# Attention state product: one full fp32 product becomes three products of split parts

## The chip, the cores and the metric

The kernel runs on one core of a Trainium2 chip. TensorE (PE) multiplies matrices, VectorE (DVE) and ScalarE (ACT) do elementwise work, GpSimd (POOL) and SyncE (SP) issue DMAs. Each engine works through its own queue in order and waits on semaphores. The metric is the device time of one execution in microseconds (us).

## The reference, cut to what matters

One layer of a hybrid backbone: a bidirectional chunkwise mLSTM (4 heads, key width 128, value width 256) and a pooling mixer, merged by sigmoid gates, then a ConvFFN. There are 128 context rows and 1024 latent rows. The part that the change touches is the output of one mLSTM step: products inside the chunk, plus the queries against the carried state:

```python
qk = jnp.einsum('bhctk,bhcsk->bhcts', qc, kc) * wts
num = jnp.einsum('bhcts,bhcsv->bhctv', qk, vc) + sc[..., None] * jnp.einsum('bhctk,bhckv->bhctv', qc, Cs)
den = jnp.sum(qk, axis=-1) + sc * jnp.einsum('bhctk,bhck->bhct', qc, ns)
```

The kernel takes the chunk as 128 rows. For each head there are 9 steps (i = 0 to 8): step 0 is the context tile, and step i takes tile i forwards (d = 0) and tile 9 - i backwards (d = 1).

## The kernel before, in words

Nearly all products are in a three-product form: an fp32 tile is rounded to fp32r ("hi", done by ACT or DVE), the rest is subtracted out on DVE ("lo", the helper `sub_hi`, L2208), and TensorE adds hi·hi, lo·hi and hi·lo. fp32r products go through in one pass. The product of the scaled queries `qs` with the state `Cst` (L1277) is the exception: it is taken in plain fp32.

The attention stage is 36 segments, one for each step e = 9h + i of the four heads. Each of them goes with one 128-column unit of the large projection ("main", 72 products of 384 columns, or the same work in 256-column pieces for values). In a segment TensorE does the scores of step i (only for i up to 4; later steps reuse cached scores in `SC`), then the main in three blocks, then `attention_values` for d = 0 and d = 1. The products of step e begin at L1273.

DVE, in each segment: the ada products of the next unit (16 operations on 128 columns, not in every segment), the lo part of a later weight unit, `gate_arguments(e + 1)` (L2350, two operations), `attention_weights(e)` (L2367 to the last `v_lo`), then `attention_outputs(e, 0)` and `(e, 1)`, which wait for the products of step e and update the state `Cst` (L2405) or, at i = 0, write the new context state `Cctx` (L2403). The products of step e wait for `attention_weights(e)`.

ACT, in each segment: the hi part of a unit, rounding of `v_hi`, then the three blocks of the main's result out of PSUM. After the first block it calls `exps()`, which takes the exponential of the gate rows of step e + 1 (L1844) and, in the segment after a head's squares were summed, the square root for that head's norm (`hm_roots`, L1808). DVE's `head_scale` (L2467) waits for this root, and it stands between `attention_weights` and `attention_outputs` of that segment (heads' steps i = 2, three times: e = 11, 20, 29). After the blocks ACT copies the scores to `SC` (L1885), and TensorE's next scores wait for that.

POOL stores `Cctx` of each head to DRAM with four DMAs (L977, L978) after step 0; in the kernel before, only the end of the kernel and the next head's write of `Cctx` wait for these stores. SP loads the gate rows `GE` of each step into one of three slots and waits for the state update three steps back.

Of the kernel before, what the change touches and what calls it, by code (L numbers as in the profile page):

```python
# [107 lines left out]
def build(nc, x_prompt, x_sample, state_C, state_n, state_m, c, c_ctx, w_ada, b_ada, g_pre_mix, g_post_mix,  # L108
# [9 lines left out]
    LS = 5  # L118
    GSLOTS = 3
    SEEN = (NT - 1) // 2  # L120
# [51 lines left out]
    loads += [("ga", d) for d in range(KD)]  # L172
    load_of = {it: w for w, it in enumerate(loads)}

    sigmoids = [it for it in loads if it[0] != "hm"]
# [86 lines left out]
    GE = place("GE", [P, GSLOTS, 2, 2, P])  # L262
    Pt_hi = place("Pt_hi", [P, 2, P], F32R)
    v_hi = place("v_hi", [P, 2, VP], F32R, at=VT0)
    v_lo = place("v_lo", [P, 2, DV], F32R, at=VT0 + (8 * VP + 31) // 32 * 32)
    a_tok = place("a_tok", [P, NT, 2, NH])
    en_tok = place("en_tok", [P, NT, 2, NH])
    ST0 = base[0]
    Cst = place("Cst", [P, 2, VW])
    Cctx = place("Cctx", [P, 2, VW])  # L270
    AT0 = base[0]
    Pt = place("Pt", [P, 2, P])
    Pt_lo = place("Pt_lo", [P, 2, P], F32R, at=AT0)
    kw_hi = place("kw_hi", [P, 2, P], F32R)
    qs = place("qs", [P, 2, P])
    SC = place("SC", [P, SEEN, 4, P])
    ada_part = place("ada_part", [P, 2, P])
    coef_rows = place("coef_rows", [32, P], at=base[0] - 1024)
# [421 lines left out]
    with nc.Block() as block:  # L700

        @block.sync
        def _(sp):
# [46 lines left out]
            for n, it in enumerate(raw_items):  # L750
                if n == 3:
                    x_load(1)
                    x_load(2)
                    mask_load()
                if n >= RS:
                    prev = raw_items[n - RS]

                    if prev[0] == "ada":
                        sp.wait_ge(ada_summed, prev[1] - ADA0 + 1)
                    else:  # L760
                        sp.wait_ge(lo_ready, prev[1] + 1)
                if it[0] == "ada":
                    src, kt = tile_cols(w_ada[0], KD, it[1] * P), KD
                else:
                    src, kt = unit_source(it[1])
                dst = raw[:, n % RS, :] if kt is None else raw[:, n % RS, 0:kt * P].rearrange("p (k c) -> p k c", c=P)
                sp.dma_start(dst, src).then_inc(landed[n % RS], 16)
                if it[0] == "unit" and 0 <= it[1] - SEG < NT * NH:
                    gates_load(it[1] - SEG)

# [169 lines left out]
        def _(pool):  # L940
# [61 lines left out]
            for w, (what, d) in enumerate(loads):  # L1002
                if w == 0:
                    pool.wait_ge(att_state, 2 * (NT * NH - 1))
                if w == 1:

                    pool.wait_ge(att_outputs, 2 * NT * NH)
                    pool.wait_ge(att_state, 2 * NT * NH)
                    pool.wait_ge(new_state_stored, 16 * 4 * NH)

                pool.wait_ge(*store_of[(what, d)])
                if w >= LS:

# [7 lines left out]
                pool.dma_start(tiles[:, w % LS, :], Z[what][d]).then_inc(tile_in[w % LS], 16)  # L1021

# [74 lines left out]
        def _(pe):  # L1097
# [159 lines left out]
            def attention_values(h, i, d):  # L1257
# [5 lines left out]
                if i == 0 and d == 0:  # L1263

                    pe.wait_ge(evac0, values_q(h))
                if i == 1 and d == 0:
                    pe.wait_ge(state_in, 64 * (h + 1))

                if e and d == 0:
# [6 lines left out]
                if i:  # L1276
                    mm = pe.matmul(ps[:, 5 + d, 0:VW], qs[:, d, :], Cst[:, d, :], start=False, stop=True)  # L1277
                if i < NT - 1:
# [313 lines left out]
        def _(act):  # L1592
# [179 lines left out]
            def sig(what, d):  # L1772
                w = load_of[(what, d)]
                act.wait_ge(tile_in[w % LS], 16 * (w // LS + 1))
                act.activation(tiles[:, w % LS, :], tiles[:, w % LS, :], ACT.Sigmoid).then_inc(sigmoids_done, 1)

# [33 lines left out]
            for m, (kind, idx) in enumerate(mains):  # L1810
# [37 lines left out]
                if kind == "q":  # L1848
                    evac_main(act, q0, qT[idx % 2], QSCALE, exps)
                elif kind == "k":  # L1850
                    evac_main(act, q0, kT[idx % 2], 1.0, exps, NB - 1 if m == SEG - 1 else 0)
                elif kind == "u":
# [11 lines left out]
                elif kind == "v":  # L1864
                    if idx == 2:

                        act.wait_ge(new_m_stored, 32)
                        act.wait_ge(g_rows_stored, 32)
                        act.wait_ge(e_rows_stored, 32)
                    for b, own in enumerate(VALUE_TILES[idx % 2]):  # L1870
                        act.wait_ge(done0, q0 + b + 1)
                        act.activation(vaug[idx // 2 % 2][:, own[0]:own[-1] + 1, 0:DV],
                                       ps[:, b, 0:len(own) * DV].rearrange("p (t c) -> p t c", c=DV), ACT.Copy).then_inc(evac0, 1)
                        if b == 0:
                            exps()
                    if idx % 2:
                        hi_split(m + 2)
                else:
                    st = stage_slot((kind, idx))
                    evac_main(act, q0, stage[st], 1.0, exps)  # L1880
                    put((kind, idx), q0 + 3)
                if seg >= 0 and 1 <= seg % NT < HALF:

                    act.wait_ge(att_weights, seg + 1)
                    act.activation(SC[:, seg % NT - 1, :, :], ps[:, 3, :].rearrange("p (a b) -> p a b", b=P),  # L1885
                                   ACT.Copy).then_inc(att_cached, 1)
# [27 lines left out]
            for d in range(KD):  # L1914
# [10 lines left out]
                act.activation(H_hi[:, k, :], tiles[:, w % LS, :], ACT.Copy).then_inc(head_hi_done, 1)  # L1925
                if d + 1 < KD and HEAD_ORDER[d + 1] >= HG:
# [271 lines left out]
        def _(dve):  # L2198
# [11 lines left out]
            def lo_split(s):  # L2210
# [5 lines left out]
                if s == S_OUT + WO - 1:  # L2216

                    dve.wait_ge(tile_used, KD + 1 + max(d for d in range(KD) if load_of[("ga", d)] % LS == LS - 1))
                hi, lo = split_of(s)
# [134 lines left out]
            def attention_weights(h, i):  # L2354
# [16 lines left out]
                if i:  # L2371
                    for d, cx in enumerate(step_tiles(i)):
                        ins = dve.tensor_tensor(qs[:, d, :], qT[v][:, cx * P:(cx + 1) * P], E[:, d, :], ALU.mult)
                for d in range(2 if i < NT - 1 else 0):
                    last = (1 - d) * (P - 1)
# [17 lines left out]
            def attention_outputs(h, i, d):  # L2393
# [10 lines left out]
                elif i < NT - 1:  # L2404
                    dve.scalar_tensor_tensor(out=Cst[:, d, :], in0=Cst[:, d, :], scalar=GE[:, e % GSLOTS, d, 1, last:last + 1],  # L2405
                                             in1=ps[:, KV_BANK[d], 0:VW], op0=ALU.mult, op1=ALU.add).then_inc(att_state, 1)
# [41 lines left out]
            def gate_branch_b(d):  # L2448

                if d == 4:  # L2450

                    dve.wait_ge(evac0, Q_P1)
                wb = load_of[("gb", d)] % LS
                dve.wait_ge(sigmoids_done, sigmoids.index(("gb", d)) + 1)
# [39 lines left out]
            for m, (kind, idx) in enumerate(mains):  # L2494
# [9 lines left out]
                if m == SEG - 1:  # L2504

                    dve.wait_ge(gate_cols_ready, 1)
                    dve.wait_ge(new_m_stored, 32)
                    dve.wait_ge(e_rows_stored, 32)
                    dve.memset(vaug[0][:, :, DV:VW], 1.0)
                    dve.memset(vaug[1][:, :, DV:VW], 1.0)  # L2510
                if m in TURN_AT:
# [35 lines left out]
            for d in range(KD):  # L2547
                k = HEAD_ORDER[d]
                wh = load_of[("o" if k >= HG else "hm", k)]
                if k >= HG:  # L2550
                    dve.wait_ge(evac0, 3 * use_of[("hm", k)] + 3)
                    dve.wait_ge(sigmoids_done, sigmoids.index(("o", k)) + 1)

                    dve.scalar_tensor_tensor(out=tiles[:, wh % LS, :], in0=stage[stage_no[("hm", k)] % 2][:, :],
                                             scalar=vT[:, V_GH + k:V_GH + k + 1], in1=tiles[:, wh % LS, :],
                                             op0=ALU.mult, op1=ALU.mult).then_inc(head_gated, 1)
# [4 lines left out]
                dve.wait_ge(head_hi_done, d + 1)  # L2561
                sub_hi(H_lo[:, k, :], tiles[:, wh % LS, :], H_hi[:, k, :]).then_inc(tile_used, 1)
            gate_branch_b(KD - 1)
            lo_split(S_BR + KD + 1)
            for d in range(KD):
                for s in SPLIT_AT[d]:
                    lo_split(s)
                wa = load_of[("ga", d)] % LS
                dve.wait_ge(sigmoids_done, sigmoids.index(("ga", d)) + 1)
# [360 lines left out]
```

## Time and profile before

| what | us |
|---|---|
| median of 3 runs | 1732.97 (1732.83 to 1733.44) |
| the profiled execution, its own time | 1731.54 |
| its span, first to last instruction | 1729.7 |
| PE busy | 1716.1 (99%) |
| DVE busy | 1265.7 (73%) |
| ACT busy | 703.4 (41%) |
| POOL busy | 256.4 (15%) |

Read it so: the durations of the trace are within the span; 1.8 us of the profiled execution lie around it, and the median of the timed runs is another 1.4 us above. The granted clock was 1.000 over the span. The attention stage lies between 177 and 725 us of the span.

### The profile page before, as it was taken

The numbers are of one execution on the slowest core, as the hardware profiler recorded it, in microseconds if no ns is written. First come the engines' busy times: TensorE is split into PE (matmuls) and PEld (weight loads), VectorE is DVE, ScalarE is ACT, GpSimd is POOL, SyncE is SP. The second block draws the span as 40 slices with busy tenths as digits, with TensorE's granted clock in tenths as the row PEclk, the third lists the DMA queues.
The fourth block names the chain that finished last, engine by engine and source line by source line (L and its number), as shares of the span: only waits on it lengthen the run. The fifth ranks groups of instructions, "written<-read, shape, count | busy, mean of one in ns | idle before, by whom it ended". The sixth has DMA issues, their size and how long they took to land.

```text
span 1729.7 us, 27434 instructions
## 1 busy us (share of the span) xinstructions
PE 1716.1 (99%) x10568; PEld 1621.7 (94%) x10568; DVE 1265.7 (73%) x2754; ACT 703.4 (41%) x1300; POOL 256.4 (15%) x255
## 2 busy tenths in 40 slices
PE   8999999999999999999999999999999999999998
PEld 3999999999999999999988899999999999888887
DVE  4777677677677777573465589888888888788998
ACT  4543222343234243461244454433344334444454
POOL 1010000100100100010000061444333333100000
PEclk9999999999999999999999999999999999999999
DMA  9214333443344455364242331333322222686876
GB/s 347 68 44 148 86 116 113 124 116 124 106 129 148 121 154 169 136 228 147 74 139 91 111 103 66 111 105 104 105 76 67 71 70 69 215 277 218 273 249 245
DMA packets 216279, 236.21 MB, mean 137 GB/s; under 512 B 11568, under 2 KB 160828, under 8 KB 216148
## 3 DMA queue, kind: packets, MB, share of 16 engines
q1 hardware_dynamic: 200916, 179.54, 34.3%
q0 software_dynamic: 10752, 38.00, 6.4%
q10 hardware_dynamic: 4480, 16.91, 2.4%
q8 instruction: 84, 1.38, 0.3%
q14 instruction: 47, 0.39, 0.1%
HBM read 181.49 MB, written 52.92 MB: 136 GB/s over the span
## 4 chain that ended last, share of the span: by engine, by line
PE 93%; DVE 3%; DMA 1%; ACT 1%; SPq 1%; issue 0%; POOL 0%; ACTq 0%; DVEq 0%; POOLq 0%
PE ps L1470 23%; PE ps L1105 13%; PE ps L1107 12%; PE ps L1106 12%; PE ps L1412 6%; PE ps L1487 5%; PE ps L1488 5%; PE ps L1489 5%; PE ps L1277 2%; PE ps L1293 2%; PE ps L1294 1%; PE ps L1295 1%; PE ps L1134 1%; PE ps L1128 1%; DMA adaw<-in_w_ada_dram 1%; PE ps L1220 1%
## 5 line engine op out<-in xcount | busy, mean ns | idle before, releaser
L1105 PE MATMUL ps<-H_hi,ring_hi 128*128 128x384 f32 x1200 | 406.1, 338 | 0.4
L1107 PE MATMUL ps<-H_hi,ring_lo 128*128 128x384 f32 x1200 | 401.8, 335 | 0.0
L1106 PE MATMUL ps<-H_lo,ring_hi 128*128 128x384 f32 x1200 | 401.8, 335 | 0.0
L1105 PEld LDWEIGHTS ps<-H_hi,ring_hi 128*128 128x128 f32 x1200 | 225.6, 188 | 1.9 <-DVE H_lo L2208 1.6
L1106 PEld LDWEIGHTS ps<-H_lo,ring_hi 128*128 128x128 f32 x1200 | 225.6, 188 | 0.2
L1107 PEld LDWEIGHTS ps<-H_hi,ring_lo 128*128 128x128 f32 x1200 | 225.4, 188 | 0.0
L1470 PE MATMUL ps<-T_hi,up_hi 128*128 128x288 f32 x608 | 130.7, 297 | 0.3 <-ACT held_g L2043 0.3
L1470 PE MATMUL ps<-T_lo,up_hi 128*128 128x288 f32 x608 | 130.4, 296 | 0.0
L1470 PE MATMUL ps<-T_hi,up_lo 128*128 128x288 f32 x608 | 130.3, 296 | 0.0
L2208 DVE TENSOR_TENSOR up_lo<-up_raw,up_hi 128x512 fp32r<-128x512 f32 x114 | 88.4, 778 | 57.2 <-ACT up_hi L2001 57.2
L2441 DVE SCALAR_TENSOR_TENSOR ada_part<-raw,condT,ada_part 128x128 f32<-128x128 f32 x448 | 120.3, 346 | 0.0
L1487 PE MATMUL ps<-B_hi,A_hi 128*128 128x512 f32 x308 | 120.1, 390 | 0.0
L1489 PE MATMUL ps<-B_hi,A_lo 128*128 128x512 f32 x308 | 120.0, 390 | 0.0
L1488 PE MATMUL ps<-B_lo,A_hi 128*128 128x512 f32 x308 | 120.0, 390 | 0.0
L1470 PEld LDWEIGHTS ps<-T_hi,up_hi 128*128 128x128 f32 x608 | 97.9, 189 | 1.1 <-ACT held_g L2043 0.5
L1470 PEld LDWEIGHTS ps<-T_lo,up_hi 128*128 128x128 f32 x608 | 98.0, 189 | 0.0
L1470 PEld LDWEIGHTS ps<-T_hi,up_lo 128*128 128x128 f32 x608 | 98.0, 189 | 0.0
L2405 DVE SCALAR_TENSOR_TENSOR Cst<-Cst,GE,ps 128x257 f32<-128x257 f32 x56 | 26.8, 479 | 97.2 <-PE ps L1281 97.2
L1470 PE MATMUL ps<-H_hi,up_lo 128*128 128x288 f32 x456 | 97.9, 296 | 0.0
L1470 PE MATMUL ps<-H_hi,up_hi 128*128 128x288 f32 x456 | 97.8, 296 | 0.0
L1470 PE MATMUL ps<-H_lo,up_hi 128*128 128x288 f32 x456 | 97.6, 296 | 0.0
L2001 ACT ACTIVATE up_hi<-up_raw 128x512 fp32r<-128x512 f32 x114 | 68.7, 620 | 69.8 <-POOL up_raw L1062 68.4
(347 smaller groups left out, 3765.9 us busy)
## 6 DMA issues: line engine op xcount, KB each, us to landing
raw<-in_w_in_dram SPq DMA_DIRECT2D x44, 512.0 KB, 4.1
up_raw<-in_w_up_dram SPq DMA_DIRECT2D x38, 512.0 KB, 5.3
w_raw<-in_w_down_dram SPq DMA_DIRECT2D x66, 256.0 KB, 3.3
raw<-in_w_ada_dram SPq DMA_DIRECT2D x32, 512.0 KB, 5.1
X<-z_f SPq DMA_DIRECT2D x44, 256.0 KB, 4.0
GE<-z_gates SPq DMA_DIRECT2D x72, 128.0 KB, 3.8
w_sub<-in_w_down_dram SPq DMA_DIRECT2D x33, 256.0 KB, 3.9
z_w_diff<-w_raw SPq DMA_DIRECT2D x22, 256.0 KB, 2.5
```

Source lines behind the costliest of these rows:

```text
L1105: pe.matmul(out, whi, xhi, start=first, stop=False)
L1106: pe.matmul(out, whi, xlo, start=False, stop=False)
L1107: return pe.matmul(out, wlo, xhi, start=False, stop=last)
L1277: mm = pe.matmul(ps[:, 5 + d, 0:VW], qs[:, d, :], Cst[:, d, :], start=False, stop=True)
L1412: mm = pe.matmul(ps[:, bank + hb, :], x[:, k, tok], w[:, hb * 512:(hb + 1) * 512], start=(n == 0 and first), stop=(n == KD - 1 and last))
L1470: mm = pe.matmul(ps[:, bank + sb, 0:SB], wt[:, w], x[:, k0 + k, cols], start=(k == 0 and n == 0), stop=(k == KD // 2 - 1 and n == 2))
L1487: pe.matmul(out, xhi, whi, start=first, stop=False)
L1488: pe.matmul(out, xhi, wlo, start=False, stop=False)
L1489: return pe.matmul(out, xlo, whi, start=False, stop=last)
L2001: act.activation(up_hi[i][:, :], src, ACT.Copy).then_inc(up_hi_done, 1)
L2208: return dve.tensor_tensor(out, full, hi.bitcast(F32), ALU.subtract)
L2441: ins = dve.scalar_tensor_tensor(out=part, in0=w, scalar=condT[:, cond, k:k + 1], in1=part, op0=ALU.mult, op1=ALU.add)
```

## The change

- `qs` and `Cst` are each split in two fp32r parts on DVE (two casts, two subtractions, four operations in every step with i > 0), and L1277 becomes three fp32r products.
- `Cst_hi` lies where `Cctx` lies, `qs_hi` in the second half of `SC[0]`, `qs_lo` over `qs`, `Cst_lo` where `v_lo` was. So DVE waits at i = 1 for the four stores of this head's `Cctx`; it also takes over TensorE's wait for the loaded state. ACT's copy of the scores at i = 1 is half as wide.
- The gate rows have 2 slots instead of 3, each load stands one unit later in SP's queue (so that it waits for the same state update as before, for the step before).
- `gate_arguments(e + 1)` moves behind `attention_weights(e)` on DVE, and ACT's `exps()` from behind the first block of the main to behind the third (`NB - 1`).
- The five tile buffers of the next stage are numbered one slot further round.

```diff
-    GSLOTS = 3
+    GSLOTS = 2
...
+    def slot(w):
+        return (w + LS - 1) % LS
...
+    v_lo = place("v_lo", [P, 2, DV], F32R)
     v_hi = place("v_hi", [P, 2, VP], F32R, at=VT0)
-    v_lo = place("v_lo", [P, 2, DV], F32R, at=VT0 + (8 * VP + 31) // 32 * 32)
+    Cst_lo = place("Cst_lo", [P, 2, VP], F32R, at=VT0 + (8 * VP + 31) // 32 * 32)
...
-    Cst = place("Cst", [P, 2, VW])
+    Cst = place("Cst", [P, 2, VP])
     Cctx = place("Cctx", [P, 2, VW])
+    Cst_hi = place("Cst_hi", [P, 2, VP], F32R, at=base[0] - 2080)
...
+    qs_lo = place("qs_lo", [P, 2, P], F32R, at=base[0] - 1024)
     SC = place("SC", [P, SEEN, 4, P])
+    qs_hi = place("qs_hi", [P, 2, P], F32R, at=base[0] - 2048 * SEEN + 1024)
...
-                if it[0] == "unit" and 0 <= it[1] - SEG < NT * NH:
-                    gates_load(it[1] - SEG)
+                if it[0] == "unit" and 0 < it[1] - SEG <= NT * NH:
+                    gates_load(it[1] - SEG - 1)
...
-                if i == 1 and d == 0:
-                    pe.wait_ge(state_in, 64 * (h + 1))
...
-                    mm = pe.matmul(ps[:, 5 + d, 0:VW], qs[:, d, :], Cst[:, d, :], start=False, stop=True)
+                    pe.matmul(ps[:, 5 + d, 0:VP], qs_hi[:, d, :], Cst_hi[:, d, :], start=False, stop=False)
+                    pe.matmul(ps[:, 5 + d, 0:VP], qs_hi[:, d, :], Cst_lo[:, d, :], start=False, stop=False)
+                    mm = pe.matmul(ps[:, 5 + d, 0:VP], qs_lo[:, d, :], Cst_hi[:, d, :], start=False, stop=True)
...
-                    evac_main(act, q0, qT[idx % 2], QSCALE, exps)
+                    evac_main(act, q0, qT[idx % 2], QSCALE, exps, NB - 1)
...
-                        if b == 0:
+                        if b == NB - 1:
                             exps()
...
-                    evac_main(act, q0, stage[st], 1.0, exps)
+                    evac_main(act, q0, stage[st], 1.0, exps, NB - 1)
...
+                    parts = 2 if seg % NT == 1 else 4
...
+                    link(ins)
+                    if i == 1:
+                        dve.wait_ge(state_in, 64 * (h + 1))
+                        dve.wait_ge(new_state_stored, 64 * (h + 1))
+                    else:
+                        dve.wait_ge(att_state, 2 * e)
+                    dve.tensor_copy(Cst_hi[:, :, :], Cst[:, :, :])
+                    link(dve.tensor_copy(qs_hi[:, :, :], qs[:, :, :]))
+                    sub_hi(Cst_lo[:, :, :], Cst[:, :, :], Cst_hi[:, :, :])
+                    ins = sub_hi(qs_lo[:, :, :], qs[:, :, :], qs_hi[:, :, :])
...
-                if 0 <= seg + 1 < NT * NH:
-                    gate_arguments(seg + 1)
+                if seg == -1:
+                    gate_arguments(0)
                 if seg >= 0:
                     h, i = seg // NT, seg % NT
                     attention_weights(h, i)
+                    if seg + 1 < NT * NH:
+                        gate_arguments(seg + 1)
                     if m - 1 in NORM_AT:
                         head_scale(NORM_AT[m - 1])
                     attention_outputs(h, i, 0)
```

`link` gives an instruction a semaphore count and makes DVE wait for it before the next one.

## Rows read from the trace of the kernel before

**Rows 1.** The page, part 4: the chain that ended last, by engine.

```profile
PE 93%; DVE 3%; DMA 1%; ACT 1%; SPq 1%; issue 0%; POOL 0%; ACTq 0%; DVEq 0%; POOLq 0%
```

**Rows 2.** Timeline of PE in step 1: start us, us, engine, line.

```profile
191.83 0.28 PE L1275 MATMUL ps<-v_hi,Pt_lo 128*128 128x258 f32 x1
191.95 0.59 PE L1277 MATMUL ps<-Cst,qs 128*128 128x257 f32 x2
...
192.50 0.28 PE L1280 MATMUL ps<-v_lo,kw_hi 128*128 128x256 f32 x1
```

**Rows 3.** Groups by line and form, DVE: busy us, mean ns | idle before.

```profile
L2288 DVE CAST H_hi<-tsc 128x384 fp32r<-128x384 f32 x40 | 14.3, 356 | 15.9 <-ACT tsc L1671 15.7
```

**Rows 4.** Timeline of DVE in segment 4.

```profile
231.54 1.21 DVE L2208 TENSOR_TENSOR ring_lo<-raw,ring_hi 128x1024 fp32r<-128x1024 f32 x1
232.67 0.60 DVE L2350 SCALAR_TENSOR_TENSOR GE<-GE,a_tok,mask 128x128 f32<-128x128 f32 x2
233.20 0.41 DVE L2367 TENSOR_TENSOR Pt<-ps,GE 128x256 f32<-128x256 f32 x1
...
233.93 0.34 DVE L2378 TENSOR_SCALAR kw_hi<-ps,GE 128x128 fp32r<-128x128 f32 x1
...
235.22 0.28 DVE L2383 CAST Pt_hi<-Pt 128x256 fp32r<-128x256 f32 x1
235.54 0.43 DVE L2208 TENSOR_TENSOR Pt_lo<-Pt,Pt_hi 128x256 fp32r<-128x256 f32 x1
```

**Rows 5.** Timelines of DVE and PE: end of the weights and first product, step 2.

```profile
205.24 0.75 DVE L2208 TENSOR_TENSOR v_lo<-vaug,v_hi 128x256 fp32r<-128x256 f32 x2
...
207.49 0.28 PE L1273 MATMUL ps<-v_hi,Pt_hi 128*128 128x258 f32 x1
```

**Rows 6.** Timelines: last store of `Cctx` and first product of step 1, heads 1, 3.

```profile
321.48 0.54 POOL L978 DMA_DIRECT2D out_dram<-Cctx  x1
...
331.01 0.28 PE L1273 MATMUL ps<-v_hi,Pt_hi 128*128 128x258 f32 x1
...
602.56 0.54 POOL L978 DMA_DIRECT2D out_dram<-Cctx  x1
...
613.09 0.28 PE L1273 MATMUL ps<-v_hi,Pt_hi 128*128 128x258 f32 x1
```

**Rows 7.** Line 978 by source: time to landing, heads 0, 1, 3 in turn.

```profile
DMA to landing us min/median/max: 8.6/10.1/11.6
...
DMA to landing us min/median/max: 7.0/8.7/10.4
...
DMA to landing us min/median/max: 8.3/10.3/12.4
```

**Rows 8.** Timelines of ACT, DVE and PE around a head's norm, segments 11 and 12.

```profile
340.95 1.28 ACT L1808 ACT_TABLE_LOAD   x1
343.96 0.21 ACT L1808 ACTIVATE hstat<-hstat 128x9 f32<-128x9 f32 x1 [1.73 <-DVE hstat L2463]
...
347.10 0.49 ACT L662 ACTIVATE qT<-ps 128x384 f32<-128x384 f32 x1 [2.55 <-PE ps L1107]
...
348.25 0.49 DVE L2405 SCALAR_TENSOR_TENSOR Cst<-Cst,GE,ps 128x257 f32<-128x257 f32 x1 [1.33 <-PE ps L1281]
...
359.40 0.76 DVE L2208 TENSOR_TENSOR v_lo<-vaug,v_hi 128x256 fp32r<-128x256 f32 x2
...
362.35 0.28 PE L1273 MATMUL ps<-v_hi,Pt_hi 128*128 128x258 f32 x1
```

**Rows 9.** Timelines of DVE and PE: the last step (35).

```profile
716.41 0.75 DVE L2208 TENSOR_TENSOR v_lo<-vaug,v_hi 128x256 fp32r<-128x256 f32 x2
...
718.21 0.28 PE L1273 MATMUL ps<-v_hi,Pt_hi 128*128 128x258 f32 x1
```

**Rows 10.** Line 1120, TensorE's first work: groups by form, then by source.

```profile
L1120 PE MATMUL ps<-reset 128*128 128x512 f32 x8 | 5.1, 797 | 2.2 <-POOL reset L946 2.2
...
L1120 PE MATMUL ps<-reset x8: 592/624/1223, 2.2 to 6.7; 128*128 128x512 f32 x8
```

More of the change, by code:

```diff
@@ L1020, in _ @@
                         pool.wait_ge(tile_used, KD + e + 1)
-                pool.dma_start(tiles[:, w % LS, :], Z[what][d]).then_inc(tile_in[w % LS], 16)
+                pool.dma_start(tiles[:, slot(w), :], Z[what][d]).then_inc(tile_in[w % LS], 16)
             pool.wait_ge(mix_sum, NB)
@@ L1774, in sig @@
                 act.wait_ge(tile_in[w % LS], 16 * (w // LS + 1))
-                act.activation(tiles[:, w % LS, :], tiles[:, w % LS, :], ACT.Sigmoid).then_inc(sigmoids_done, 1)
+                act.activation(tiles[:, slot(w), :], tiles[:, slot(w), :], ACT.Sigmoid).then_inc(sigmoids_done, 1)
             def value_rounding(h, i):
@@ L1848, in _ @@
                 if kind == "q":
-                    evac_main(act, q0, qT[idx % 2], QSCALE, exps)
+                    evac_main(act, q0, qT[idx % 2], QSCALE, exps, NB - 1)
                 elif kind == "k":
-                    evac_main(act, q0, kT[idx % 2], 1.0, exps, NB - 1 if m == SEG - 1 else 0)
+                    evac_main(act, q0, kT[idx % 2], 1.0, exps, NB - 1)
                 elif kind == "u":
@@ L1884, in _ @@
                     act.wait_ge(att_weights, seg + 1)
-                    act.activation(SC[:, seg % NT - 1, :, :], ps[:, 3, :].rearrange("p (a b) -> p a b", b=P),
+                    parts = 2 if seg % NT == 1 else 4
+                    act.activation(SC[:, seg % NT - 1, 0:parts, :], ps[:, 3, 0:parts * P].rearrange("p (a b) -> p a b", b=P),
                                    ACT.Copy).then_inc(att_cached, 1)
@@ L1924, in _ @@
                     act.wait_ge(head_gated, k - HG + 1)
-                act.activation(H_hi[:, k, :], tiles[:, w % LS, :], ACT.Copy).then_inc(head_hi_done, 1)
+                act.activation(H_hi[:, k, :], tiles[:, slot(w), :], ACT.Copy).then_inc(head_hi_done, 1)
                 if d + 1 < KD and HEAD_ORDER[d + 1] >= HG:
@@ L2216, in lo_split @@
                 if s == S_OUT + WO - 1:
-                    dve.wait_ge(tile_used, KD + 1 + max(d for d in range(KD) if load_of[("ga", d)] % LS == LS - 1))
+                    dve.wait_ge(tile_used, KD + 1 + max(d for d in range(KD) if slot(load_of[("ga", d)]) == LS - 1))
                 hi, lo = split_of(s)
@@ L2404, in attention_outputs @@
                 elif i < NT - 1:
-                    dve.scalar_tensor_tensor(out=Cst[:, d, :], in0=Cst[:, d, :], scalar=GE[:, e % GSLOTS, d, 1, last:last + 1],
+                    dve.scalar_tensor_tensor(out=Cst[:, d, 0:VW], in0=Cst[:, d, 0:VW], scalar=GE[:, e % GSLOTS, d, 1, last:last + 1],
                                              in1=ps[:, KV_BANK[d], 0:VW], op0=ALU.mult, op1=ALU.add).then_inc(att_state, 1)
@@ L2452, in gate_branch_b @@
                     dve.wait_ge(evac0, Q_P1)
-                wb = load_of[("gb", d)] % LS
+                wb = slot(load_of[("gb", d)])
                 dve.wait_ge(sigmoids_done, sigmoids.index(("gb", d)) + 1)
@@ L2508, in _ @@
                     dve.wait_ge(e_rows_stored, 32)
+                    dve.memset(Cst[:, :, VW:VP], 0.0)
                     dve.memset(vaug[0][:, :, DV:VW], 1.0)
@@ L2552, in _ @@
                     dve.wait_ge(sigmoids_done, sigmoids.index(("o", k)) + 1)
-                    dve.scalar_tensor_tensor(out=tiles[:, wh % LS, :], in0=stage[stage_no[("hm", k)] % 2][:, :],
-                                             scalar=vT[:, V_GH + k:V_GH + k + 1], in1=tiles[:, wh % LS, :],
+                    dve.scalar_tensor_tensor(out=tiles[:, slot(wh), :], in0=stage[stage_no[("hm", k)] % 2][:, :],
+                                             scalar=vT[:, V_GH + k:V_GH + k + 1], in1=tiles[:, slot(wh), :],
                                              op0=ALU.mult, op1=ALU.mult).then_inc(head_gated, 1)
@@ L2561, in _ @@
                 dve.wait_ge(head_hi_done, d + 1)
-                sub_hi(H_lo[:, k, :], tiles[:, wh % LS, :], H_hi[:, k, :]).then_inc(tile_used, 1)
+                sub_hi(H_lo[:, k, :], tiles[:, slot(wh), :], H_hi[:, k, :]).then_inc(tile_used, 1)
             gate_branch_b(KD - 1)
@@ L2567, in _ @@
                     lo_split(s)
-                wa = load_of[("ga", d)] % LS
+                wa = slot(load_of[("ga", d)])
                 dve.wait_ge(sigmoids_done, sigmoids.index(("ga", d)) + 1)
```

## The prediction

> **What bounds the kernel.** I first read the chain that ended last: TensorE holds 93% of it, DVE 3% [rows 1]. The reader is to see that time comes off only where TensorE's own work shrinks, and is lost wherever TensorE is made to wait. Then TensorE's timeline in the attention stage: products follow each other without a gap, and the only thing that could stop them in a segment is a late `attention_weights`. So the second view is each segment's margin: from the end of the last `v_lo` on DVE to the first product (L1273). It is 1.50 in step 2 [rows 5], the smallest of the ordinary segments; elsewhere it lies between 1.8 and 5.7, and in the very last step it is 1.05 [rows 9]. The third view is what the new waits look at: the landing of POOL's stores [rows 6, 7], and ACT's table load and root around a norm [rows 8].
>
> **TensorE's saving.** From the start of L1277 to the start of L1280 is 0.55, and in it lie the fp32 product and one single-pass product [rows 2]. Two single-pass products start 0.12 apart [rows 2]. The fp32 product so costs 0.43, its three replacements 0.36: 0.07 saved, in 4 heads x 8 steps x 2 directions = 64 products, 4.5 us. TensorE is the bound here, so all of it counts. The bounds are 0.06 and 0.08 a product, 3.8 to 5.1.
>
> **DVE's new work.** An operation that the next one doesn't wait for overlaps it: the 1024-column subtraction lasts 1.21 but the next starts after 1.13; a linked one costs its duration and some 0.04 (the cast of 0.28 takes 0.32) [rows 4]. The extra link on `qs` is then 0.12. Casts: 0.28 for 256 columns, 0.356 for 384 [rows 3, 4], so 0.43 for 516, of which 0.34 count; the linked `qs_hi` 0.32. Subtractions: 0.43 for 256 and 1.21 for 1024 columns [rows 4], less the overlap 0.34 and 1.13, so `Cst_lo` (516) 0.61 and `qs_lo` 0.34. Sum 1.73 a step; if the wide cast went no faster than the subtraction, 2.0. The two gate arguments, 0.53 from 232.67 to 233.20 [rows 4], leave the time ahead of the weights, so the weights end 1.20 later. TensorE arrives 0.07 sooner relative to DVE's start. 1.50 - 1.27 leaves 0.23 in step 2 [rows 5]: the cover for nearly all of this is DVE's idle time behind the weights, and it costs nothing. Without the cover it would be up to 1.3 a step. In step 35 nothing moves out (there are no further arguments), so 1.73 + 0.07 + 0.05 for the handing over stand against 1.05 [rows 9]: TensorE waits 0.8.
>
> **The wait for the stores, the largest term.** At i = 1 DVE may cast the state only when all four stores of this head's `Cctx` have landed, since `Cst_hi` lies on it. The last is issued at 321.48 in head 1 and lands 10.4 later, 331.88 [rows 6, 7]. TensorE wants the finished weights at 331.01 [rows 6]. Behind the waiting instruction are queued on DVE: the four operations (1.61), the `kw` parts (233.93 to 235.22, 1.29), the `Pt` parts (0.32 and 0.34) and `v_lo` (0.76) [rows 4, 8], 4.32, and some 0.15 (my estimate from the link's 0.12) for waking and handing over. TensorE can start at 336.35, 5.3 late. In heads 0 and 2 the last store is also issued 9.5 before the product as in head 1; it lands 11.6 later in head 0 [rows 7] and 10.4 in head 2. These give 11.6 + 4.47 - 9.52 = 6.5 and 5.3. In head 3: 602.56 + 12.4 + 4.47 - 613.09 = 6.3 [rows 6, 7]. Together 23.4. Nothing hides it: ACT, TensorE's blocks and SP all run dry. Bounds: a landing 1 us sooner or later each time, 19 to 28.
>
> The Trainium skill's DMA: Bandwidth & Descriptors (Anatomy of one DMA) fits a GpSimd-issued transfer as 2.0 us plus size over bandwidth. By that, a 0.5 KB store would land 2 us after its issue, far ahead of TensorE, and this term would be nothing. The rows say 10.4 to 12.4. The same page says that the semaphore waits for the write's receipt, and that this can be surprisingly long to HBM, with which the trace agrees.
>
> **The root moved behind the third block.** In segments 11, 20 and 29 `hm_roots` is called in `exps()`. Before, the table load ran at 340.95, under the main, and the root at 343.96 waited only for DVE [rows 8]. Now ACT first takes the third block at 347.10, starts the exponential some 0.39 later and holds 0.43 for it, then loads the table (1.28) to 349.20 and takes the root there instead of at 343.96 [rows 8]. From the root's start to the end of the nine scalings it was 348.25 - 1.33 - 343.96 = 2.96 [rows 8], so scaling ends at 352.1 and `attention_outputs` starts there instead of at 348.25: 3.85 late. Behind it on DVE stand the state update, the ada products, a lo split and the next weights. The next products had a margin of 362.35 - 360.16 = 2.19 [rows 8]. 3.85 + 1.20 + 0.14 + 0.05 - 2.19 = 3.05 lost. In segment 29 TensorE meets it sooner, at the head transposes, which wait for the same scaling, and its margin is smaller: 3.4. Together 9.5; bounds 7 to 11.
>
> **The rest.** `exps()` behind the third block delays ACT's copy to `SC`, which TensorE's scores await, by up to 0.33; where the main is a value unit that eats the margin: three times 0.1. Where the exponential also needs its table again (segments 12, 21) TensorE is already waiting for the weights. The gate loads keep the same waits one step on and land some 6 us before the moved arguments need them; the buffers' new numbers move no transfer. 0.3 together, 0 to 2.
>
> **TensorE's clock.** Four waits of 5 to 6.5 us are longer than any idle time of TensorE after its start in this trace. At the start, coming from rest, its first eight products took 797 on average against 592 for the fastest [rows 10], about 1.6 us more in all, as at the lower of its two clock levels, 1.2 GHz, before 2.4. If three of the four waits drop the clock and each return costs 1.3 to 1.6, that is 4; bounds 0 and 12 (four times 3).
>
> The Trainium skill's TensorE: Matmul & The Clock Gate (Part 1) says that the slow level is the default and sustained activity lifts it, so idle time brings it back. That no wait of this length stands in the trace means that no run here shows it yet.
>
> **Sum.** On the profiled execution's 1731.5: -4.5 + 0.8 + 23.4 + 9.5 + 0.3 + 4.0 = +33.5, 1765.0. The median of the timed runs is 1.4 above that execution; the same on top gives 1766.5, which I round to 1766.
>
> **Rivals.**
> - *The stores land in time* (they take the few us that nearby loads take, or the landings are read too late). For: the trace's stores carry only 128 and 0.5 KB. Against: landings in sequence, in all four heads. Only the norm stays: 1766 - 23 - 4 = 1739. It decides when the last landing is under 5 us after issue. 0.05.
> - *The root is not late*: ACT reaches it early enough, the stores alone count: 1757. It decides at a margin of 5 in the segment behind. 0.05.
> - *Not slower: lateness on DVE never reaches TensorE*. The one mechanism is the margin ahead of L1273: were it over 6.5 in steps 1 and 3 of each head, all delays would vanish behind the mains and 1733 - 4.5 = 1728.5 be left. The margins of [rows 5, 8] speak against it. 0.03.
> - *DVE becomes the bound in ordinary segments too*: with operations of 2.4 in place of 1.73 the margins of about 0.6 in some ten segments and 0.2 in step 2 go, and step 35 loses more, 3 to 8: 1770 to 1775, more if segments follow each other late. 0.09.
> - *The clock stays down longer after each wait*, up to 3 us a time: 1774, and above 1776 with long landings. 0.08.
> - The forecast, with its own range of 1759 to 1773: 0.70.
>
> Faster or slower by under 0.2% is about what a measurement of this kernel can tell from no change. Only the third rival lies at or below it: faster 0.03, same 0.01, slower 0.96. The range of 8 in 10 leaves out the first and third rival and the far ends of the last two: 1756 to 1776.
>
> **What the profile after should show.** L1277's successors start 0.12 apart. DVE sits idle some 6.5 us inside `attention_weights` ahead of `Cst_hi` at i = 1, ended by the stores, and TensorE idle 5.3 to 6.5 ahead of L1273 there, four times. The table load of the root starts behind the third block, `attention_outputs` of segments 11, 20 and 29 starts about 5.2 after the first product instead of 1.35, and TensorE waits about 3 before step 3 (in segment 29 before the transposes). Wait of 0.8 at the last step. Ordinary segments have a margin of 0.2 to 1.8. The granted clock may show short falls behind the four waits. Wrong would be: `Cst_hi` not waiting, or stores landing within 5 us; more than ten other segments in which TensorE waits.

## The result and the profile after

The changed kernel takes 1772.42 us (median of 5 runs, 1771.37 to 1776.35) against 1733.44 for the kernel before (1732.83 to 1734.85) in the same session: a ratio of 1.0225, 95% interval 1.0214 to 1.0236. It is slower by 39.0 us; 1766 with a range of 1756 to 1776 was forecast. The profiled execution took 1771.95, its span 1770.1: 40.4 more than the span before.

The chain that ended last, in the changed kernel (TensorE held 93% of it before, DMA 1% [rows 1]):

```profile
PE 87%; DVE 6%; DMA 4%; ACT 1%; SPq 1%; issue 1%; POOL 0%; DVEq 0%; ACTq 0%
```

TensorE's waits in the changed kernel (what waits, for whom: us in total, times, longest). In the kernel before no line of the attention's products stands in this view.

```profile
PE ps L1277 <- DVE v_lo L2215: 28.1, 7, 7.7
PE ps L1315 <- DVE hm L2484: 3.0, 1, 3.0
...
PE ps L1260 <- ACT SC L1892: 1.6, 2, 0.8
```

L1277 is the first product of a step. Its seven waits are the four steps 1, two of the three steps behind a norm, and the last step. The wait of the third norm is met earlier, at the head's transposes (L1315).

**Step 1 of head 0**, timeline of DVE, then of TensorE, changed kernel:

```profile
195.18 0.43 DVE L2387 CAST Cst_hi<-Cst 128x516 fp32r<-128x516 f32 x1 [9.14 <-DMA out_dram<-Cctx]
...
196.79 0.34 DVE L2395 TENSOR_SCALAR kw_hi<-ps,GE 128x128 fp32r<-128x128 f32 x1
...
198.74 0.76 DVE L2215 TENSOR_TENSOR v_lo<-vaug,v_hi 128x256 fp32r<-128x256 f32 x2
```

```profile
199.55 0.58 PE L1277 MATMUL ps<-v_hi,Pt_hi 128*128 128x258 f32 x1 [7.74 <-DVE v_lo L2215]
199.93 0.41 PE L1278 MATMUL ps<-v_lo,Pt_hi 128*128 128x256 f32 x1
200.14 0.42 PE L1279 MATMUL ps<-v_hi,Pt_lo 128*128 128x258 f32 x1
200.36 0.42 PE L1281 MATMUL ps<-Cst_hi,qs_hi 128*128 128x258 f32 x1
```

DVE idles 9.14 us until the stores of `Cctx` have landed; from the cast to TensorE's product pass 4.37. The four new operations take 1.61 (195.18 to 196.79), as worked out. The stores, line 985 by source, heads 0 and 1 (the larger number of a row is the last store's way to its landing; it was 11.6 and 10.4 before [rows 7], and is 10.6 in head 2 and 11.7 in head 3):

```profile
DMA to landing us min/median/max: 8.9/10.9/12.9
...
DMA to landing us min/median/max: 8.3/9.3/10.3
```

**The clock.** From the second on, the products above lie 0.21 and 0.22 apart, those of step 3 below 0.12 (the first one behind a wait takes longer in both). Stretches of the changed kernel (us from:to, length; PE, PEld, DVE, ACT and POOL busy; PEclk, the granted clock; DMA share and GB/s):

```profile
196.70:203.30 6.60, 3.75 (x17) 3.75 (x18) 4.52 (x16) 2.58 (x4) 0.00 (x0) 0.50 0.00 0
...
343.40:350.20 6.80, 5.12 (x24) 5.12 (x25) 4.25 (x16) 4.45 (x15) 0.00 (x0) 0.50 0.38 154
493.60:500.40 6.80, 3.87 (x18) 3.88 (x19) 4.64 (x16) 3.27 (x10) 0.00 (x0) 0.50 0.42 166
643.70:650.60 6.90, 3.94 (x18) 3.95 (x19) 4.68 (x16) 3.28 (x13) 0.00 (x0) 0.51 0.22 89
203.50:343.30 139.80, 136.39 (x917) 136.18 (x915) 111.54 (x376) 31.59 (x71) 5.46 (x10) 1.00 0.38 107
```

In each of the four steps 1 the clock is granted at half, 1.2 GHz, for some 6.8 us, and stands at 2.4 GHz between them. Each fall begins while TensorE still waits: the first products stand at 199.55, 345.08, 496.53 and 646.65. What is left of the falls behind them is 3.9, 5.1, 3.9 and 3.9 us, and their price, in the table below, is a little under half of that.

**The norm of head 0**, timeline of ACT, then of DVE (before, the root ran at 343.96 and `attention_outputs` at 348.25, 1.35 behind the first product [rows 8]):

```profile
363.43 0.49 ACT L669 ACTIVATE qT<-ps 128x384 f32<-128x384 f32 x1 [3.67 <-PE ps L1114]
363.82 0.41 ACT L1850 ACTIVATE GE<-GE 128x256 f32<-128x256 f32 x1
364.25 1.28 ACT L1814 ACT_TABLE_LOAD   x1
365.54 0.21 ACT L1814 ACTIVATE hstat<-hstat 128x9 f32<-128x9 f32 x1
```

```profile
366.04 2.46 DVE L2484 TENSOR_SCALAR hm<-hm,hstat 128x256 f32<-128x256 f32 x9
368.40 0.48 DVE L2422 SCALAR_TENSOR_TENSOR Cst<-Cst,GE,ps 128x257 f32<-128x257 f32 x1
```

The first product stands at 363.24, `attention_outputs` 5.16 behind it (5.2 was forecast). The step behind, on TensorE:

```profile
381.57 0.39 PE L1277 MATMUL ps<-v_hi,Pt_hi 128*128 128x258 f32 x1 [1.77 <-DVE v_lo L2215]
...
382.03 0.28 PE L1281 MATMUL ps<-Cst_hi,qs_hi 128*128 128x258 f32 x1
382.15 0.29 PE L1282 MATMUL ps<-Cst_lo,qs_hi 128*128 128x258 f32 x1
382.27 0.29 PE L1283 MATMUL ps<-Cst_hi,qs_lo 128*128 128x258 f32 x1
382.39 0.28 PE L1285 MATMUL ps<-v_hi,kw_hi 128*128 128x258 f32 x1
```

The three replacements of the fp32 product take 0.36 (382.03 to 382.39); before, 0.55 less 0.12 [rows 2].

**An ordinary segment and the last step**, step 2 of head 0 and segment 35:

```profile
215.85 0.76 DVE L2215 TENSOR_TENSOR v_lo<-vaug,v_hi 128x256 fp32r<-128x256 f32 x2
...
217.12 0.28 PE L1277 MATMUL ps<-v_hi,Pt_hi 128*128 128x258 f32 x1
...
756.97 0.39 PE L1277 MATMUL ps<-v_hi,Pt_hi 128*128 128x258 f32 x1 [0.63 <-DVE v_lo L2215]
```

In step 2 a margin of 0.51 is left (217.12 - 216.61) where 0.23 was worked out from 1.50 [rows 5]; in the versions below whose clock doesn't fall there it is 0.2 to 0.4. In the last step TensorE waits 0.63.

**Where the 40.4 us went**, from the first products of the 36 segments in both traces (how much later each comes than before, and by how much that grows from one to the next):

| place | forecast | measured |
|---|---|---|
| ahead of segment 0 | 0 | +0.1 (1.14 up to there, with an early fall of the clock, and -1.06 for a wait that went) |
| steps 1: wait for the stores | 23.4 | 7.9, 5.3, 5.6, 5.7 = 24.5 |
| steps 1: clock at half | 4.0 | 1.8, 2.4, 1.8, 1.8 = 7.8 |
| norms | 9.5 | 3.0, 3.0, 3.35 = 9.4 |
| last step | 0.8 | 0.8 |
| TensorE's products | -4.5 | -4.0 (0.063 each, from the ordinary steps: 0.12 to 0.15 a step) |
| elsewhere | 0.3 | 0.2 |
| the last 100 us | 0 | 1.6 |

The last row (one wait of 0.5 for `A_lo` from DVE, and steps of 0.1) is not the change's: in the traces below, with nothing edited there, it lies between -0.1 and 1.7, and the 1.7 is that of the kernel before with one wait added on TensorE.

### The profile page after: what moved, and what is told of

It reads as the page before. It is cut to its first block, busy times and chain, and to the rows that moved or that the text cites. A ratio compares the mean times of both kernels' runs of the same rounds, so it can differ in the third digit from the quotient of the medians.

```text
span 1770.1 us, 27719 instructions
## 1 busy us (share of the span) xinstructions
PE 1724.5 (97%) x10632; PEld 1629.2 (92%) x10632; DVE 1318.9 (75%) x2883; ACT 700.2 (40%) x1300; POOL 257.3 (15%) x255
## 4 chain that ended last, share of the span: by engine, by line
PE 87%; DVE 6%; DMA 4%; ACT 1%; SPq 1%; issue 1%; POOL 0%; DVEq 0%; ACTq 0%
PE ps L1476 23%; PE ps L1112 12%; PE ps L1114 12%; PE ps L1113 12%; PE ps L1418 6%; PE ps L1493 4%; PE ps L1495 4%; PE ps L1494 4%; DMA out_dram<-Cctx 3%; PE ps L1299 1%; PE ps L1301 1%; PE ps L1300 1%; PE ps L1141 1%; DMA adaw<-in_w_ada_dram 1%; PE ps L1135 1%
## 5 line engine op out<-in xcount | busy, mean ns | idle before, releaser
L669 ACT ACTIVATE stage<-ps 128x384 f32<-128x384 f32 x72 | 35.3, 490 | 186.2 <-PE ps L1114 186.2
```

The costliest lines, as they stand in the source:

```text
L669: act.activation(dst[:, b * BW:(b + 1) * BW], ps[:, b, 0:BW], ACT.Copy, scale=scale).then_inc(evac0, 1)
```

## The experiments

Every kernel was compared with runs of the kernel before on its own chip; a median is given with that one beside it.

### 1. A buffer of its own for the state's high part at step 1

```
+    Cst_hi1 = place("Cst_hi1", [P, 2, VP], F32R, at=base[0] - 2048 * (SEEN - 1))
...
                     if i == 1:
                         dve.wait_ge(state_in, 64 * (h + 1))
-                        dve.wait_ge(new_state_stored, 64 * (h + 1))
...
+                    if i == 2:
+                        dve.wait_ge(new_state_stored, 64 * (h + 1))
+                    C_hi = Cst_hi1 if i == 1 else Cst_hi
-                    dve.tensor_copy(Cst_hi[:, :, :], Cst[:, :, :])
+                    dve.tensor_copy(C_hi[:, :, :], Cst[:, :, :])
```

At step 1 the part lies in room of `SC` that is free then, and the wait for the stores moves one step on.

> The changed kernel, but at i = 1 the hi part of the state goes to a place of its own (the cached scores of steps 2 and 3, unused then), so that DVE no longer waits there for the stores of Cctx; it waits for them at i = 2 instead, when they have long landed. My theory (idle time of TensorE behind the stores, and the clock that falls because of it): the four waits of 24.5 in all go, and with them the four clock falls that cost 7.9: 1772.4 - 32.4 = 1740.0. Rival A (the clock falls come from the new mix of work, not from the waits): only the waits go, 1748, and the granted clock still falls four times. Rival B (DVE's longer work is the true limit at step 1 and the stores only hid it): TensorE still waits there, above 1750.

Measured: 1740.7 (before: 1734.37), ratio 1.0040 [1.0026, 1.0054]. TensorE's waits:

```profile
PE ps L1278 <- DVE v_lo L2217: 4.2, 3, 1.8
PE ps L1317 <- DVE hm L2488: 3.0, 1, 3.0
```

The four waits at step 1 are gone (margins there 1.1 to 1.3) and their clock falls with them; the norms' waits stay as they were (behind the third of them this trace has a fall of the clock of its own, see experiment 7). One wait and one shared buffer account for some 32 of the 39 us.

### 2. The roots behind the first block again

```
+            if b == 0 and first:
+                first()
...
+                def roots():
                     if m - 1 in NORM_AT:
                         hm_roots(NORM_AT[m - 1])
...
-                    evac_main(act, q0, qT[idx % 2], QSCALE, exps, NB - 1)
+                    evac_main(act, q0, qT[idx % 2], QSCALE, exps, NB - 1, roots)
```

> The changed kernel, but the root of a head's norm is taken by ACT behind the first block of the main again; the exponential stays behind the third. My theory (the root behind the third block is what makes the scaling and all behind it late): the waits of TensorE in segments 11 to 12, 20 to 21 and 29 to 30 go, 9.4 in all, 1763.0; attention_outputs of these segments starts 1.3 after the first product. Rival (the lateness comes from the exponential and the copy of the scores behind the third block): at most 3 of the 9.4 come back, 1769 or more.

Measured: 1763.81 (before: 1734.37), ratio 1.0167 [1.0153, 1.0181].

```profile
PE ps L1279 <- DVE v_lo L2219: 22.3, 5, 6.8
...
PE ps L1262 <- ACT SC L1896: 1.4, 2, 0.7
```

The mirror image: the steps 1 keep their waits, no segment behind a norm waits for its weights. What is left there is 0.7 for ACT's copy of the scores. Of the norms' 9.4, 7.4 come back in the trace and not all, as the theory had it. The ratio falls by 10 us because the stores also landed sooner here: the steps 1 lose 22.2 in place of 24.5.

### 3. Both, and the last step as well

`both` makes the two edits. `both_last` also moves the lo halves of the last pool groups on DVE behind the last weights:

```
+                    else:
+                        pooled_lo(m - 1)
...
+                    if m + 1 < NM - 1:
+                        pooled_lo(m)
```

> Both edits at once: the hi part of the state apart at i = 1, the root behind the first block. My theory (the rest of the change is TensorE's saving of 0.063 a product, 64 times, less 0.8 at the last step, and all else is covered by DVE's idle time): before - 4.1 + 0.8 = before - 3.3, 1730.1. Rival (DVE's 1.73 more a step makes it the bound in ordinary segments once the long waits no longer give it time): a wait of 0.2 to 1 in ten or more segments, 1733 to 1740.

> Both edits, and DVE subtracts the lo halves of the last two pool groups behind the last attention_weights, no longer ahead of them (2.5 of work). My theory (the last step is late by DVE's work ahead of it alone): the 0.8 at the last step goes, before - 4.1, 1729.3. Rival (the lo halves are now late for the branch products behind the main): 0 to 2 slower than both.

Measured (before: 1734.37): `both` 1731.42, 0.9984 [0.9975, 0.9993]; `both_last` 1730.99, 0.9982 [0.9973, 0.9991]. In the second the last step has a margin again and its 0.8 us are gone in the trace; the times can't tell the two apart. Both have this left (`both`, waits of TensorE, then ACT's timeline around the norm of head 0):

```profile
PE ps L1263 <- ACT SC L1898: 1.4, 2, 0.7
```

```profile
345.10 0.49 ACT L670 ACTIVATE qT<-ps 128x384 f32<-128x384 f32 x1 [0.78 <-PE ps L1117]
345.61 1.28 ACT L1854 ACT_TABLE_LOAD   x1
346.90 0.42 ACT L1854 ACTIVATE GE<-GE 128x256 f32<-128x256 f32 x1
347.23 0.58 ACT L1898 ACTIVATE SC<-ps 128x512 f32<-128x512 f32 x1
```

Behind the root the exponential must load its table again, 1.28, and now it stands ahead of the copy to `SC`, which the scores await. Each of the two costs 0.8 to 1.0 from one first product to the next.

### 4. The exponential behind the copy

```
-                    evac_main(act, q0, stage[st], 1.0, exps, NB - 1, roots)
+                    evac_main(act, q0, stage[st], 1.0, lambda: None, NB - 1, roots)
...
+                exps()
```

> The version with the buffer kept apart, the roots behind the first block and the last step's low halves late, and with the next segment's exponentials issued behind ScalarE's copy of the scores instead of ahead of it. Theory: the two waits of 0.7 us ahead of the scores of segments 12 and 21 (1.0 each from first product to first product) and three of 0.2 at the scores of step 2 go, 2.6 in all less what of them comes back elsewhere: about 4 us less than before, 0.9977 of it. Rival: the exponentials are now late for the weights of the next block, and what is saved at the scores is lost there: 0.998 or more, no better than the version that it starts from.

Measured: 1728.19 (before: 1732.83), ratio 0.9972 [0.9961, 0.9983]. The line of the copy is no longer among the waits, segments 12 and 21 come no later than ordinary ones, and the view has no new wait in the attention stage (segments 30 and 31 come 0.2 later each, why stays open). The span is 3.4 below the one before, 2.4 below that of `both_last`. This is the fastest version: with its buffers and ACT's order mended, the change is a gain of 0.3%. By the trace the 36 segments give 3.6 of it, TensorE's products; 1.1 more is the wait ahead of segment 0, which SP's new order saves (the missed steps, further down) and not the products, and an early fall of the clock takes 1.5 back.

### 5. Why the stores land so late

`no_small_stores` is the changed kernel without the stores of the normalizer column (four bytes a partition): that output stays unwritten, and the waits count the large stores alone.

```
-                    pool.dma_start(new_n[0, 0, d, h].rearrange("(r c) -> r c", c=1), Cctx[:, d, DV:VW]).then_inc(new_state_stored, 16)
...
-                        dve.wait_ge(new_state_stored, 64 * (h + 1))
+                        dve.wait_ge(new_state_stored, 32 * (h + 1))
```

> The changed kernel without the small stores of the normalizer (four bytes a partition); that output is left unwritten, and the waits count the large stores alone. Theory A: the small stores are what lands late; the last large one of a head lands about 5 us behind its issue, the four waits at step 1 shrink to 1 us or less and the clock falls behind them go: 1740 to 1745. Theory B: the large stores land as late without them, behind the loads of the next block on the same DMA engines: landing stays near 10 us behind the issue, and the time at 1765 to 1772.

Measured: 1740.96 (before: 1732.83), ratio 1.0046 [1.0030, 1.0061]. The last large store lands 5.8 us behind its issue in head 0, 7.1 in head 1, 4.9 and 4.2 in the others; only head 1 is still late at step 1, by 1.0. So the small stores are what makes the landing late. No run stores the same 0.5 KB in longer rows: that it is the four-byte rows, and not two more transfers, is not shown.

`small_apart` writes every output. It copies the two normalizer columns into a tile of their own, stores them behind both large ones on a semaphore of their own, and DVE waits for the large ones alone. `small_first` only changes the order: both small ones, then both large ones.

```
+                    dve.tensor_copy(nctx[:, d:d + 1], ps[:, KV_BANK[d], DV:VW])
...
-                    pool.dma_start(new_n[0, 0, d, h].rearrange("(r c) -> r c", c=1), Cctx[:, d, DV:VW]).then_inc(new_state_stored, 16)
+                for d in range(2):
+                    pool.dma_start(new_n[0, 0, d, h].rearrange("(r c) -> r c", c=1), nctx[:, d:d + 1]).then_inc(new_n_stored, 16)
```

> The changed kernel, all outputs written, with the two normalizer columns of a head copied into a buffer of their own and stored from it on a semaphore of their own, behind the two large stores. VectorE's wait at step 1 then stands for the large stores alone. Theory (a small store takes some 4 us, and whatever is issued behind it on the queue lands later by as much): the large pair lands 4.2 to 7.1 us behind the issue of its second, as without small stores, and the time is that of the kernel without them, 1738 to 1745. Rival (what holds up the large stores is the traffic of the small ones on the DMA engines, in whatever order): the waits at step 1 stay at 3 us or more each, 1755 or more.

> The changed kernel with a head's four stores in another order: both small ones, then both large ones; the wait counts all four, as in the changed kernel. Theory (the sum of the four on one queue sets the last landing): 10 to 13 us behind the first issue as now, 1768 to 1776. Rival (a small store is slow only behind a large one): the last lands about 7 us behind its issue, 1741 to 1755.

Measured (before: 1734.95): `small_apart` 1769.45, 1.0196 [1.0179, 1.0213]; `small_first` 1770.10, 1.0209 [1.0189, 1.0228]. The theory that I had written for the first has fallen, its rival stands: the large stores land late although nothing small is issued ahead of them. With `small_first` the time and the last landing (12.3 to 12.6 us behind the first issue) came as its theory had them, but `small_apart` refutes the reason given, a sum along one queue. The first small store of `small_first`, with no other store ahead of it, itself takes 7.9 us to land in head 0 and 5.4 to 6.5 in the others; a first large one takes 3.3 to 5.4 in the other traces. Time to landing of the large stores of head 0, `no_small_stores`, then `small_apart`:

```profile
DMA to landing us min/median/max: 4.6/5.2/5.8
```

```profile
DMA to landing us min/median/max: 4.6/8.6/12.6
```

And it is not only the stores. The 512 KB loads issued around them in head 0, `no_small_stores` (178 to 192), then `small_apart` (181 to 195), there with the small stores; the last column is the median us to landing:

```profile
raw<-in_w_ada_dram SPq DMA_DIRECT2D x1, 512.0 KB, 5.9
raw<-in_w_in_dram SPq DMA_DIRECT2D x1, 512.0 KB, 3.8
```

```profile
raw<-in_w_ada_dram SPq DMA_DIRECT2D x1, 512.0 KB, 12.7
raw<-in_w_in_dram SPq DMA_DIRECT2D x1, 512.0 KB, 10.1
...
out_dram<-nctx POOLq DMA_DIRECT2D x2, 0.5 KB, 10.9
```

Two transfers of 0.5 KB hold up the megabyte around them by 5 to 8 us in head 0, on another queue too, wherever they stand in the order (`small_first`: 11.0 and 9.0); the load beside the stores of the other heads lands 2 to 6 us later with them. The kernel before has it as well (11.6 and 10.1 for the same two loads), where nothing waits for it. The Trainium skill's DMA: Bandwidth & Descriptors (Specifications) says that a write under 512 bytes is done as a read, a change and a write back. That the small stores are costlier than their size agrees with this, but no run here shows the mechanism. Why loads into the chip's own memory suffer too stays open.

### 6. The wait alone, and where it stands

To the kernel before, only a wait for the four stores is added at step 1: on DVE ahead of the key parts, or on TensorE ahead of its first product.

```
+                if i == 1:
+                    dve.wait_ge(new_state_stored, 64 * (h + 1))
```

```
+                    pe.wait_ge(new_state_stored, 64 * (h + 1))
```

> The kernel before, with one wait added: at step 1 of each head VectorE waits for the head's last store of the old state ahead of the key parts. Theory (the store lands 10 to 13 us behind its issue, and the place of the wait in VectorE's order is what costs): the state part that TensorE's first product needs comes 2.7 us behind the landing, so that the four steps are late by about 4.9, 3.7, 3.7 and 4.8: 17 in all, and up to 2 more for each where the clock falls behind it; 1750 to 1758. Rival (the store has landed before VectorE comes there): 0, the time before.

> The kernel before, with the same wait put on TensorE instead, ahead of its first product of step 1. Theory: it stands for the landing alone, 2.1, 0.9, 0.9 and 1.9 us behind the time at which that product starts now: 5.8 in all, and no fall of the clock: about 1739. Rival (the landing is in time): 0.

Measured (before: 1735.38): on DVE 1757.32, 1.0137 [1.0118, 1.0156]; on TensorE 1742.93, 1.0043 [1.0028, 1.0058]. On DVE the steps 1 come 4.3, 4.2, 3.8 and 3.7 later, 16.0 (17 expected), and 7.5 more are lost behind them, each time with the clock at half. On TensorE they come 2.5, 1.0, 2.5 and 1.0 later, 7.0, and the clock falls once, behind one of the two waits of 2.5, for 1.7. So the second theory held for the landing (5.8 expected) and not for the clock, of which it expected no fall. The landing accounts for 7 us, the place of the wait for 9 more, and the clock comes on top. One waiting instruction costs what is queued behind it on its engine.

### 7. What brings the clock down

No transfer is waited for here, and the stores and loads run as in the other versions: to `both`, copies of the state are added on DVE at step 1, each waiting for the last, 14 of them or 7.

```
+                    for _ in range(14 if i == 1 else 0):
+                        link(dve.tensor_copy(C_hi[:, :, :], Cst[:, :, :]))
```

> The version with both repairs, and 14 more copies of the state queued on VectorE at step 1 of each head, each waiting for the last, so that TensorE's first product of that step waits though no transfer is late. 14 copies of about 0.47 are 6.6 us, less the 1.3 of room that step has: a wait of 5.3 in each of four heads, 21 in all. Theory (idle time of TensorE alone makes the clock fall): the clock halves after each wait, for about 6.8 us, at about 2 each: 21 + 8 = 29 over the version without the copies. Rival (the fall comes with the late store and its transfers): granted clock 1.0 throughout, 21 over it.

> The same with 7 copies: 3.3 less 1.3 is a wait of 2.0 in each head, 8 in all. Theory: idle time so short does not bring the clock down (the waits of 3.0 us behind the head's normalization were followed by a fall in one place of nine only): 8 over the version without the copies. Rival: it falls here too, at about 2 each: 16 over it.

Measured (before: 1732.83): 14 copies 1762.08, 1.0167 [1.0152, 1.0183]; 7 copies 1742.53, 1.0054 [1.0040, 1.0068]. TensorE's waits at step 1 are 5.3 and 2.0 long as meant. The stretches there, 14 copies (all four heads), then 7 copies (first and last of four; the granted clock is 1.00 in the two between as well):

```profile
196.80:200.20 3.40, 3.19 (x15) 3.20 (x16) 1.46 (x7) 2.58 (x4) 0.00 (x0) 0.50 0.00 0
340.10:347.00 6.90, 4.84 (x22) 4.84 (x23) 4.37 (x16) 4.18 (x14) 0.00 (x0) 0.51 0.29 118
490.30:497.10 6.80, 6.01 (x28) 6.01 (x29) 4.25 (x16) 5.29 (x18) 0.00 (x0) 0.50 0.16 63
637.10:643.90 6.80, 4.09 (x19) 4.09 (x20) 4.43 (x16) 3.42 (x13) 0.00 (x0) 0.50 0.21 87
```

```profile
195.00:211.00 16.00, 15.55 (x98) 15.50 (x99) 14.72 (x48) 4.33 (x9) 0.00 (x0) 1.00 0.35 90
...
622.00:638.00 16.00, 15.53 (x98) 15.53 (x99) 11.63 (x39) 9.32 (x28) 0.00 (x0) 1.00 0.43 132
```

Idle time of TensorE alone brings the clock down, whatever it waits for. At the four waits of 5.3 it fell four times, at 1.3 to 2.7 us each, 7.9 together; at the four of 2.0 never. In all traces: every step 1 that came 3.7 us or more late, 24 of them, had a fall, of two of 2.5 one, of five of 3.0 at a norm's transposes two (it cost 2.7 in `store_apart`). By the ratios 14 copies cost 32 us over `both` and 7 copies 12; by the traces 29 and 10, with 1.3 and 3.0 in them for early falls in the first 50 us that the trace of `both` hasn't. Those early falls stand beside waits of at most 1.5 us, so the length of one wait doesn't settle it everywhere; what else counts stays open.

## Why the prediction was right, step by step

- **TensorE's saving** was right in its mechanism; 0.063 a product and not 0.07, 4.0 and not 4.5.
- **DVE's work** was right: the four operations take 1.61, and what is left of the margins is 0.5 in step 2 and 0.7 where it was 2.0. No ordinary segment waits. The last step loses the 0.8 that was worked out.
- **The wait for the stores** was the largest term and right to 1.1 in 24.5. The 4.32 queued behind the waiting cast are the reason why a landing 0.8 to 3.4 us too late for TensorE becomes 5 to 8 (4.37 measured, with the waking). Part of the fit is luck: head 0's landing came later than the row that it was read from (12.9 and not 11.6), head 3's sooner (11.7 and not 12.4). The rival that the stores land in time is refuted by the four rows. It is what the fit in the Trainium skill's DMA: Bandwidth & Descriptors (Anatomy of one DMA) would have given. Experiment 5 says what this fit leaves out here: the small stores. It also shows that the long way to HBM, with which the prediction explained the landing, is at most a part of it: without them the large stores to HBM land in 4.2 to 7.1.
- **The root** was right: 3.0, 3.0, 3.35 for 3.05, 3.05, 3.4. In the first two norms it comes in two waits, 0.8 at the scores and 1.8 at the product, and not in one; that the sum is right is in part luck, for the forecast had put nothing on the scores here, and a wait of 0.7 stays there when the root is mended.
- **The clock** is the term that was mis-sized. I let three of four waits drop it, at 1.3 to 1.6 each, and no row showed how many would; all four did, and stayed at half for 6.8 us, at 1.8 to 2.4 each: 7.8 and not 4. The price came from TensorE's first eight products, where it rises once from rest. In step 1 the clock already falls during the wait and stays low after it. That the Trainium skill's TensorE: Matmul & The Clock Gate (Part 1) makes the slow level what idle time brings back agrees with experiment 7.
- **Two steps were missed, both small.** I wrote that in segments 12 and 21 the exponential's table load meets a TensorE that waits anyway. That holds only while the root is late: once it isn't, the load costs 0.8 to 1.0 each time (experiments 2 to 4). And a gain was missed: ahead of segment 0 TensorE waited for ACT, which waited for DVE's gate arguments; in the changed kernel both waits are gone, 1.1 less. DVE was late because its weights were: in SP's queue the first gate rows stood ahead of their load, which was issued at 138.73. With the gate rows one unit later it is issued at 122.14, and DVE no longer waits for it. Kernel before, TensorE, ACT and DVE:

```profile
160.35 2.17 PE L1345 MATMUL ps<-mixed,wpool 128*128 128x384 f32 x6 [0.84 <-ACT stage L1764]
```

```profile
159.32 0.42 ACT L1844 ACTIVATE GE<-GE 128x256 f32<-128x256 f32 x1 [1.22 <-DVE GE L2350]
```

```profile
144.49 0.48 DVE L2437 TENSOR_SCALAR ada_part<-raw,condT 128x128 f32<-128x128 f32 x2 [6.57 <-DMA raw<-in_w_ada_dram]
```

By the measured terms the sum is 0.1 + 24.5 + 7.8 + 9.4 + 0.8 - 4.0 + 0.2 + 1.6 = 40.4, 6.9 above the forecast's 33.5: the clock 3.8, the last 100 us 1.6, the stores 1.1, TensorE's saving 0.5. So the range held, but with its largest miss in the term that rested on the least.

## What to carry to other kernels

A buffer laid over one that is still being stored puts a DMA's landing into an in-order engine's queue: before sharing it, read the landing of the last store, add all that is queued behind the waiting instruction, and hold that against the margin of the engine that sets the end. Here one such buffer cost 32 us and hid, with the late roots, a gain of 3, and of some 5 once the exponentials stood behind the copy. When an activation that needs another table moves behind one that an engine waits for, or ahead of it, both directions of the table switch have to be priced. And where a wait of several us is put on TensorE, add some 2 us for its clock (1.3 to 2.7 here).

## What was not expected of the hardware

- Two stores of 0.5 KB, four bytes a partition, make two 512 KB loads on another queue land later (12.7 in place of 5.9, 10.1 in place of 3.8), whether they are issued ahead of the large stores or behind them.
- Of the falls of the clock some lasted 3.4 us and some 6.8, and one wait of 2.5 was followed by a fall and one not. In the first 50 us there were none, one or two of them, in kernels with the same work there, at 1.3 to 1.7 us each. The time of the kernel before varies with its clock: over 46 runs it rises from 1731.9 where the mean granted clock is 1.000 to 1735.6 where it is 0.997. Where in those runs the clock fell isn't known.
